# Query and key/value phase of a decoder step: rotary halves twice in the weights, values by token, squares summed before the matrix product, key tiles between the heads

## What is computed

```python
proj = einsum('btd,de->bte', x, w_in)                 # 384 query, 256 latent, 32 rotary key columns, and more
q = einsum('btr,re->bte', rms_norm(c_q, q_norm_g), w_uq)   # 16 heads x (64 plain + 32 rotary)
q_nope, q_pe = q[..., :64], apply_rope(q[..., 64:], pos)   # [x1 cos - x2 sin, x2 cos + x1 sin]
c_kv = rms_norm(c_kv, kv_norm_g)
k_pe = apply_rope(k_pe, pos)
kv = einsum('bsc,ce->bse', c_kv, w_ukv)               # 16 heads x (64 key + 64 value), prompt tokens only
```

## Time and profile before

| | |
|---|---|
| median of 3 runs | 3173.14 us (3171.33 to 3176.74) |
| the profiled execution | 3172.03 us, span 3170.2 us |
| TensorE matmul busy | 2978.9 us, 94% of the span |
| VectorE, GpSimd, ScalarE busy | 1558.7, 1016.8, 756.7 us |
| mean granted TensorE clock | 0.964 |

### The profile page before, as it was taken

The page is one execution under the profiler, slowest core; times in us unless marked ns, Lnnn a source line. Parts: engine busy times, 40 slices in busy tenths (PEclk is TensorE's granted clock), DMA queues, the critical chain, the costliest instruction groups (busy, mean ns, idle before and its releaser), DMA issues.

```text
span 3170.2 us, 46396 instructions
## 1 busy us (share of the span) xinstructions
PE 2978.9 (94%) x19012; PEld 2626.6 (83%) x19012; DVE 1558.7 (49%) x2120; ACT 756.7 (24%) x1151; POOL 1016.8 (32%) x546
## 2 busy tenths in 40 slices
PE   7889999999999999999999978999889999999996
PEld 7767999989998995555677668899789999999995
DVE  1661677774746464555344467665352222222226
ACT  1111121253535353545323110100120000000003
POOL 3331333332323322444211113344323333433330
PEclk9999999999999997999899989999999999999997
DMA  4134223555746445222343323353201111111101
GB/s 131 39 112 125 83 82 117 153 148 143 178 135 177 139 121 151 60 60 69 130 179 141 111 92 108 103 170 115 61 31 44 47 40 46 40 46 40 46 20 55
DMA packets 313405, 308.22 MB, mean 97 GB/s; under 512 B 31094, under 2 KB 271995, under 8 KB 310779
## 3 DMA queue, kind: packets, MB, share of 16 engines
q1 hardware_dynamic: 249768, 190.26, 21.3%
q10 hardware_dynamic: 59914, 78.22, 7.4%
q0 software_dynamic: 3584, 37.75, 3.1%
HBM read 227.97 MB, written 78.20 MB: 97 GB/s over the span
## 4 chain that ended last, share of the span: by engine, by line
PE 68%; DVE 12%; issue 9%; POOL 4%; DMA 3%; ACT 2%; SPq 1%; ACTq 0%; POOLq 0%; DVEq 0%
PE ps L859 41%; PE ps L1025 10%; POOL pr L805 4%; PE ps L1358 2%; PE ps L1301 2%; PE ps L1261 2%; PE ps L1274 2%; DVE cv L1956 2%; DVE flo L2445 1%; PE ps L1278 1%; PE ps L933 1%; PE ps L1104 1%; DVE cv L1950 1%; PE ps L1058 1%; DMA gt<-d_z 1%
## 5 line engine op out<-in xcount | busy, mean ns | idle before, releaser
L737 POOL TENSOR_TENSOR whi<-raw,cst 128x1024 fp32r<-128x1024 f32 x172 | 334.0, 1942 | 1404.9 <-PE ps L859 1273.1
L739 POOL TENSOR_TENSOR wlo<-raw,whi 128x1024 fp32r<-128x1024 f32 x172 | 469.5, 2730 | 13.5
L859 PE MATMUL ps<-ahi,whi 128*128 128x352 f32 x1824 | 400.2, 328 | 51.7 <-DVE alo L2316 21.5
L859 PE MATMUL ps<-alo,whi 128*128 128x352 f32 x1824 | 398.2, 327 | 0.0
L859 PE MATMUL ps<-ahi,wlo 128*128 128x352 f32 x1824 | 395.0, 325 | 0.0
L859 PEld LDWEIGHTS ps<-ahi,whi 128*128 128x128 f32 x1824 | 313.5, 191 | 58.7 <-issue 34.5
L859 PEld LDWEIGHTS ps<-ahi,wlo 128*128 128x128 f32 x1824 | 314.9, 190 | 0.0
L859 PEld LDWEIGHTS ps<-alo,whi 128*128 128x128 f32 x1824 | 313.6, 189 | 0.0
L1025 PE MATMUL ps<-xhi,whi 128*128 128x352 f32 x768 | 257.3, 335 | 0.6 <-ACT xraw L1534 0.4
L1025 PE MATMUL ps<-xlo,whi 128*128 128x352 f32 x768 | 248.8, 324 | 0.0
L1025 PE MATMUL ps<-xhi,wlo 128*128 128x352 f32 x768 | 248.8, 324 | 0.0
(11 more groups left out here) (320 smaller groups left out, 5015.8 us busy)
## 6 DMA issues: line engine op xcount, KB each, us to landing
raw<-in_w_in SPq DMA_DIRECT2D x61, 512.0 KB, 5.0
s_a<-d_acum SPq DMA_DIRECT2D x32, 512.0 KB, 7.1
d_xbc<-so ACTq DMA_DIRECT2D x24, 528.0 KB, 2.7
gt<-d_g SPq DMA_DIRECT2D x24, 528.0 KB, 3.7
raw<-in_w_ffn_gate SPq DMA_DIRECT2D x22, 512.0 KB, 3.7
raw<-in_w_ffn_up SPq DMA_DIRECT2D x22, 512.0 KB, 3.7
raw<-in_w_ffn_down SPq DMA_DIRECT2D x22, 512.0 KB, 3.5
d_z<-zo ACTq DMA_DIRECT2D x16, 528.0 KB, 5.0
```

Of the source, the lines that this page charges most:

```text
L737: pool.tensor_tensor(whi[s][:, :], raw[:, u], ones[:, 0:1].broadcast_to([P, UNIT]), ALU.mult).then_inc(sem("unit_hi"), k["unit_hi"].adds(1))
L739: pool.tensor_tensor(wlo[s][:, :], raw[:, u], whi[s][:, :].bitcast(F32), ALU.subtract).then_inc(sem("unit_split"), k["unit_split"].adds(1))
L859: last = pe.matmul(ps[0:m, 3 * b + c, 0:width], w(j), x[:, j, at:at + width], start=i == 0, stop=i == n - 1)
```

## The change

What it does, part by part:

- The splits of the query units lay each head out in 128 columns: 64 plain, 32 rotary, and the 32 rotary once more with their halves swapped. The small unit is loaded so by five transfers in place of four. The sine table has its sign in it and stands on partitions 96 to 127. The f32 `turn` is gone; `rotate` multiplies both copies out of PSUM and adds.
- The splits of the key/value units put keys and values apart. A key product is two heads' keys; values are computed with the tokens' tile as the stationary operand, 256 columns of values at a time, so they come by token, and `turn_values` is gone.
- Squares of a norm are added on VectorE first and multiplied by ones once.
- Key tiles stand between the query pairs from pair 3 on, on TensorE, VectorE and ScalarE; the latent's norm stands on VectorE after pair 1 and its lower halves after pair 2.
- Bank sets alternate by use (`bank_set`). Query and key/value loops are written out. One loop of four units at a later product (ahi, alo) is too; a few semaphores are named anew.

```diff
-    rope[1, NOPE:QH] = np.tile(np.sin(ang), (2, 1))
+    rope[1, QH:QH + half], rope[1, QH + half:P] = -np.sin(ang), np.sin(ang)
...
-                     (part(2), tile_of(w_in, C_PE, 32)), (part(3), tile_of(w_in, C_PE, 32))])
+                     (part(2), tile_of(w_in, C_PE, 32))] +
+                    [(lambda r, h=h: part(3)(r)[:, :, 16 * h:16 * h + 16], tile_of(w_in, C_PE + 16 * (1 - h), 16)) for h in range(2)])
...
+        def split_queries(u, s):
...
+            pool.wait_ge(sem("unit_done"), k["unit_done"].next())
+            src = raw[:, u % RAW, 0:6 * QH].rearrange("p (a n) -> p a n", n=QH)
+            hi, lo = (t[s][:, 0:6 * P].rearrange("p (a n) -> p a n", n=P) for t in (whi, wlo))
+            parts = ((slice(0, QH), slice(0, QH)), (slice(QH, QH + 16), slice(NOPE + 16, QH)), (slice(QH + 16, P), slice(NOPE, NOPE + 16)))
+            for dst, at in parts:
+                last = pool.tensor_tensor(hi[:, :, dst], src[:, :, at], ones[:, 0:1].unsqueeze(2).broadcast_to([P, 6, at.stop - at.start]), ALU.mult)
...
+            for dst, at in parts:
+                last = pool.tensor_tensor(lo[:, :, dst], src[:, :, at], hi[:, :, dst].bitcast(F32), ALU.subtract)
...
+        def split_keys_and_values(u, s):
...
+            src = raw[:, u % RAW].rearrange("p (k h c n) -> p k h c n", k=2, h=4, n=NOPE)
+            hi, lo = (t[s][:, :].rearrange("p (k c h n) -> p k h c n", k=2, h=4, n=NOPE) for t in (whi, wlo))
+            for j in range(2):
+                last = pool.tensor_tensor(hi[:, j], src[:, j], ones[:, 0:1].unsqueeze(2).unsqueeze(3).broadcast_to([P, 4, 2, NOPE]), ALU.mult)
...
+        def keys_and_values(s):
...
+            for half in range(2):
+                b = bank_set(1)
+                view = lambda t: lambda j: t[:, j * 512 + half * P:j * 512 + (half + 1) * P]
+                last = products(b, view(hi), view(lo), kn_hi, kn_lo, 2, [(0, 512), (512, 512)])
+                last.then_inc(sem("sub_done"), k["sub_done"].adds(1))
+                for t in range(4 * half, 4 * half + 4):
...
+                    for i in range(6):
+                        j, part = divmod(i, 3)
+                        x, w = ((kn_hi, hi), (kn_lo, hi), (kn_hi, lo))[part]
+                        last = pe.matmul(ps[:, VBANK[t // 2], t % 2 * 256:t % 2 * 256 + 256], x[:, j, t * P:(t + 1) * P], w[:, j * 512 + 256:(j + 1) * 512],
+                                         start=i == 0, stop=i == 5)
...
+        for u in range(6):
+            if u == 5:
+                sum_rows(0)
+            dense(u, bank_set(1), xhi, xlo, KT, wait_free=False)
+        for p in range(8):
+            query_pair(p)
+            if p == 0:
+                sum_rows(1)
+            for i in range(2 * (p - 3), min(2 * (p - 3) + 2, 9)) if p >= 3 else ():
+                key_tile(i)
...
+        def rotate(p):
+            for h, b in enumerate((1, 0) if p == 0 else (0, 1)):
...
+                dve.tensor_tensor(thirds(rot[b][R0:R1]), ps[R1:R2, 3 * b:3 * b + 3, 0:CH], thirds(rope_t[R1:R2, 1]), ALU.mult).then_inc(step.sem, step.adds(1))
+                dve.tensor_tensor(thirds(qh[b][R0:R1]), ps[R0:R1, 3 * b:3 * b + 3, 0:CH], thirds(rope_t[R0:R1, 0]),
+                                  ALU.mult).then_inc(sem(f"out_free{b}"), k[f"out_free{b}"].adds(1))
...
+                dve.tensor_tensor(qh[b][R0:R1], qh[b][R0:R1], rot[b][R0:R1], ALU.add).then_inc(sem("q_turned"), k["q_turned"].adds(1))
...
+        for p in range(8):
+            rotate(p)
+            if p == 1:
+                norm("kn", 1, 6, 1, ckv, 2, V_KVN)
+            elif p == 2:
+                lower("kn", ckv, kn_lo, kn_hi, 2)
+            for i in range(2 * (p - 3), min(2 * (p - 3) + 2, 9)) if p >= 3 else ():
+                key_tile(i)
```

More of the change, by code:

```diff
@@ L884, in turn @@
-        def turn(b, src):
-            for c, (at, width) in enumerate(all_tokens):
[L887 to L896, removed]
@@ L926, in _ @@
             last.then_inc(sem("keys_turned"), k["keys_turned"].adds(1))
-        pe.wait_ge(sem("keys_out"), k["keys_out"].next(2))
-        def turn_values(b):
-            pe.wait_ge(sem(f"v_free{b}"), k[f"v_free{b}"].held())
-            for j in range(SEQ // P):
-                last = pe.matmul(ps[:, 6 + b, j * VH:(j + 1) * VH], kvh[b][:, j * P:(j + 1) * P], ident[:, NOPE:P],
-                                 start=True, stop=True)
-            last.then_inc(sem("v_turned"), k["v_turned"].adds(1))
@@ new lines, in _ @@
+        for u in range(6):
[8 more added lines that the diff above has]
+                key_tile(i)
+        pe.wait_ge(sem("kn_split"), k["kn_split"].next(2))
+        pe.wait_ge(sem("keys_out"), k["keys_out"].next(2))
+        for s in range(4):
+            keys_and_values(s)
@@ L1521, in _ @@
-            for b in range(2):
-                act.wait_ge(sem(f"v_free{b}"), k[f"v_free{b}"].next())
-                act.dma_start(d_v[bass.ds(i * 4 + pair * 2 + b, 1)].rearrange("a p n -> (a p) n"), vst[b]).then_inc(sem(f"v_stored{b}"), k[f"v_stored{b}"].adds(16))
+                h = 4 * s + 2 * half
+                act.dma_start(d_k[h:h + 2].rearrange("a p n -> (a p) n"), kvh[b]).then_inc(sem(f"k_stored{b}"), k[f"k_stored{b}"].adds(16))
+            act.wait_ge(sem("v_read"), k["v_read"].next(4))
@@ L1902, in _ @@
+        dve.wait_ge(sem("out_free1"), 1)
+        square(0, cq[:, 0])
+        dve.wait_ge(sem("out_free0"), 2)
+        square(1, cq[:, 1])
+        add_squares(0, False)
+        dve.wait_ge(sem("out_free1"), 2)
+        square(1, cq[:, 2])
+        add_squares(0, True)
+        dve.wait_ge(sem("sq_ready"), k["sq_ready"].same())
         dve.wait_ge(sem("vecs_ready"), 2)
-        norm("qn", 1, 0, cq, qn_lo, qn_hi, 3, V_QN)
+        norm("qn", 1, 3, 0, cq, 3, V_QN)
+        lower("qn", cq, qn_lo, qn_hi, 3)
@@ L1904, in _ @@
         dve.wait_ge(sem("rope_full"), k["rope_full"].next(32))
-        rotate(1, small[R0:R1, :], "key_turned")
-        square(4, 0)
-        norm("kn", 0, 1, ckv, kn_lo, kn_hi, 2, V_KVN)
-        dve.wait_ge(sem("kn_split"), k["kn_split"].same())
-        with looped(dve, 8, {k["out_free0"]: 2, k["out_free1"]: 2, k["rot_ready"]: 2, k["dve_step"]: 2, k["q_turned"]: 2}):
-            for b in range(2):
-                k[f"out_free{b}"].n += 1
-                rotate(b, qh[b][R0:R1], "q_turned")
@@ L1913, in _ @@
-        for i in range(9):
+        dve.wait_ge(sem("qn_split"), k["qn_split"].same())
+        dve.tensor_tensor(rot[0][R0:R1], small[R1:R2, :], rope_t[R1:R2, 1], ALU.mult).then_inc(step.sem, step.adds(1))
+        dve.tensor_tensor(small[R0:R1, :], small[R0:R1, :], rope_t[R0:R1, 0], ALU.mult).then_inc(step.sem, step.adds(1))
+        dve.wait_ge(step.sem, step.same())
+        dve.tensor_tensor(small[R0:R1, :], small[R0:R1, :], rot[0][R0:R1], ALU.add).then_inc(sem("key_turned"), k["key_turned"].adds(1))
```

280 lines of the change are left out of this document (148 added, 132 removed).

## The result

The changed kernel took 3098.07 us (median of 4 runs, 3091.57 to 3101.50), the kernel before 3172.74 beside it: a ratio of 0.9764, 95% interval 0.9748 to 0.9779. It is 2.4% faster, 74.7 us; 3106 was forecast. The profiled execution took 3096.15 us, its span 3094.3.

A forecast was written before the change was run, and what follows sets the result against it. TensorE, at 94% of the span, was taken as the bound. Terms -65.2 + 0.6 - 2.6 + 0.3 + 0.5 gave -66.4 us, the order of time -67.7; -67 was taken, for 3106 us, range 3090 to 3122.

The forecast's parts named there:

- VectorE isn't late: Rival, queries: collisions fall on GpSimd, two TensorE waits and their slow starts shrink; -12 us, 3094; chance 0.15.
- order of time: Engine-by-engine timeline of the phase: convolution starts at 254.9 us in place of 322.58, or -67.7 us.
- The sum of terms: Whole phase: work removed, products, waits, clock and transfer add to -65.2 + 0.6 - 2.6 + 0.3 + 0.5 = -66.4 us.
- Start: First query pair, after the query norm on VectorE: begins at 104.0 and not 122.28; TensorE waits 1.6 us.
- Pairs 0 and 1: Queries: pair 0 ends at 112.8, TensorE waits 6.9 us for a bank set, pair 1 starts at 123.6.
- Pair 3: Queries: bank set comes free at 149.5, after VectorE's latent norm; TensorE waits 7.4 us; ends with two key tiles at 160.8.
- Pairs 4 to 7: Later queries with key tiles: TensorE needs 9.9 us per pair, VectorE 9.4, so VectorE isn't waited for.
- The ninth tile's copy: Before the key/value loop: TensorE waits 4.4 us for this VectorE copy behind the last rotation, until 204.0.
- Everything after the phase follows TensorE unchanged: Rest of the kernel behind the changed phase: follows TensorE, with no gain or cost of its own.
- short matmuls don't pay: Rival, value products: 256-column matmuls take 0.163 us each; +8.3 us, 3114; chance 0.1.
- the splits become the bound: Rival, GpSimd splits: about 16 us each would eat the 67 us gain; 3173 and more; slower or nothing 0.05.
- VectorE sets the pace: Rival, queries: more VectorE collisions, 20 to 24 us, start the loop 10 us later; 3116; chance 0.15.

The follow-up runs named there:

- a_q_wide: Changed kernel with each head's scratch and store at 128 rows in place of 96; 3100.30 us, ratio 0.9773 to the kernel before.
- a_no_recip: Changed kernel without the reciprocal of the latent's norm on VectorE (that value is wrong); 3089.77 us, ratio 0.9750 to the kernel before.
- a_tiles_act: Changed kernel with the nine key tiles copied out of PSUM by ScalarE in place of VectorE; 3093.01 us, ratio 0.9747 to the kernel before.
- a_split_twice: Changed kernel with GpSimd doing both halves of each query split twice; 3108.69 us, ratio 0.9801 to the kernel before.
- a_best: Changed kernel with the edits of a_tiles_act and a_q_wide, latent's squares on ScalarE, latent's norm cut into pieces between heads; 3086.32 us, ratio 0.9728.
- a_best2: a_best with stores of 96 rows again and the key tiles' stores issued ahead of the heads'; 3092.73 us, ratio 0.9754 to the kernel before.

## Why the prediction was right, and what was off

The mechanism held, and the likeliest case with it: 3098 in a range of 3090 to 3122. The median alone wouldn't tell, as it lies nearer to the 3094 of "VectorE isn't late"; the waits decide: 22.6 us for 21.1, in the places that were named and one more (2.60 before pair 1). Off are 8 us: 2.5 in the phase (69.5 where I took 67) and 6.3 behind it, less 0.8 because the median lay 1.9 and not 1.1 above the profiled execution.

| term | forecast | measured |
|---|---|---|
| turns | 17 x 1.87 = 31.8 | 16 x 1.90 = 30.4 and the key's |
| value turns | 27.9 | 27.9 |
| a value matmul of 256 columns | 0.120 (0.109 to 0.163) | 0.114 |
| key and value products | 45.6 | 8 x (2.76 + 2.73) = 43.9 |
| TensorE's waits | 21.1 | 22.6 |
| small unit in five transfers | +0.5 (0 to 2.0) | first product at 28.27 and 27.95, before 28.39 and 28.60: none seen, within a scatter of 1.9 |
| query split, key/value split | 4.2, 4.7 | alone 3.95 and 4.64 (219.36 to 224.00); beside VectorE 4.9 to 9.4 and 5.6 |
| start of the convolution | 254.9 | 253.0 |

- **A slip of 2 us.** By the order of time the loop starts at 204.0, and 204.0 + 45.6 + 0.8 is 250.4. The prediction has 252.4 and then adds 2.0 for the slow start, which was in it already. Added up rightly the order of time gives 252.9, against 253.0 measured, and -69.7 us against -69.5. That it fits to 0.1 us is luck, as starts of one program up to the first pair differ by 3 us. Within it two errors cancel: the loop began 2.0 late (206.51 against 204.5 with the transfer's 0.5) and took with its slow start and last wait 46.5 for 48.4.
- **The sum of terms** gave -66.4, 3.1 short. Products that were 1.7 us quicker and a transfer whose cost isn't seen make 2.2 of it, the turns 0.5; the waits' gain was 1.6 and not 2.6, the other way; that leaves some 1.4 for the sums of squares and slow starts, which I can't split further.
- **Start.** The first pair waited 3.1 us, not 1.6, as unit 5 ended 0.6 early and the first lower part took 2.20 us where I had 1.2. GpSimd's first piece of unit 7's split, begun at 101.93 and 1.69 long, was in its way (102.54 is when the lower part starts in the row). The Trainium skill ("SBUF — State Buffer", Who interferes with whom) says that the two exclude each other for whole instructions when VectorE has two SBUF inputs and GpSimd reads SBUF; the trace agrees, in both directions: the lower part takes 1.0 us more, about what was left of GpSimd's piece when it began (102.54 to 103.62), and GpSimd's three pieces take 4.33 for 1.75.
- **Pairs 0 and 1.** I had given no slow start to pair 0; it took 11.5 us for 8.7. Thereby the wait for the second sum of squares was 2.58 and not 6.9, and the sum started at 119.00 (forecast 119.7). Pair 1 waited 2.60 more, for its bank set, in place of a slow start, and came at 123.64 (forecast 123.6). A slow start ahead of a wait for VectorE was free here: in a_q_wide pair 0 has no slow start, the wait for the sum is 5.8 us, and nothing is won.
- **Pair 3.** Waited 8.57 for 7.4, forecast start 149.5, measured 151.36. That VectorE's latent norm makes this wait is shown by a_no_recip, where it is 1.30.
- **Pairs 4 to 7** came 9.84 us apart (9.9 forecast). TensorE sets the pace, with little to spare: VectorE needs about 9.6, among it a wait of 0.6 for ScalarE's copy of the first head (L1508), which I had not seen. That adds up in the queue: the last tile's copy was 2.4 us later than forecast.
- **Loop.** "The ninth tile's copy" was the right cause, at 4.86 for 4.4: a_tiles_act took 3.7 of it away.
- **Behind the phase.** "Everything after the phase follows TensorE unchanged" was wrong, and of the signs of being wrong one did show: a later stage has grown, the feed-forward stretch, by 6 to 11 us. It is hidden in the sum, as the stretches ahead of it got shorter. No cost or gain of this kind stood in the forecast, so part of its distance of 8 us is two things not foreseen that nearly cancel.

The rivals: that short matmuls don't pay fell (0.114). The Trainium skill ("TensorE: Matmul & The Clock Gate", Back-to-back issue gap) would make 109 ns of 256 columns by its formula and 216 of 512, where the rows show 114 and 230; its sustained 131 ns at 512 isn't reached in this stream, in which each matmul has a weight load of its own. That the splits become the bound fell in a_split_twice. "VectorE sets the pace" and "VectorE isn't late" both fell as whole cases, but the first holds in part: turns of 30.4 us were worth 23.2, since VectorE's norms now stand in TensorE's way, and relieving VectorE won 12.7 and 14.9 us of the phase, counted from the first pair.

**What stays open** is the rest of the kernel. Its 2841 us in both profiles of the changed kernel stand against 2848 and 2851 before, but eight more kernels with the changed kernel's code there gave 2844.9 to 2849.0. Why the feed-forward loop waits once per round, where nothing but the program ahead of it was edited, and why the stretches ahead of it got shorter, no run shows. The missing 4.8 us wait at the end of the convolution is no gain of the change, as nine of the ten profiles with that code have it. The medians differ by 73 to 75 us, so some 4 to 5 us of them lie outside the phase, a net of the two; whether that net is more than chance isn't shown. If it isn't, the change is worth the 69.5 us of its phase, 2.2%.

## What to carry to other kernels

TensorE work that is moved into the weights' layout counts one for one where TensorE's stretch is full, and only in part where it waits for VectorE; read busy against length for the stretch before and think of the one after, too. When TensorE gets shorter, look at once at what VectorE does between two releases of a PSUM bank, and cut long pieces (a 6.75 us reciprocal) up or give them to an idle ScalarE: here the edits of a_best together shortened the phase by 13 us more, and the median by 11 (a_best2, with the phase 2 us shorter still, had a median only 5 lower). A wait taken from the middle of a queue comes back in part at the next one, so price the last wait of the stage and not the one that looks longest; and add up the order of time twice.

## What the runs showed of the hardware

- A matmul of 256 columns in fp32r with a weight load of its own takes 0.114 us, one of 512 columns 0.230, one of 352 0.162 (0.485 for three): time is nearly in proportion to columns down to 256.
- A wait of the same length doesn't always bring a slow start. After 3.10 us of wait the first pair took 11.5 us in the changed kernel and 8.9 in a_best (103.43 to 112.3), with the same work of TensorE before it; after 2.15 us it took 10.5 in a_tiles_act and 8.9 in a_q_wide.
- Three instructions of GpSimd that take 1.75 us alone took 4.33 beside three lower parts of VectorE, which took 4.84 in place of 3.59: both lose.
- The same code behind the phase took 2841.3 to 2849.0 us in ten profiles (all of changed kernels but a_no_recip), a scatter as large as most single edits here are worth. Below some 10 us the stage's own length in the profile tells more than the median of four runs.
